# Asking for ScalarE's rounding of a weight unit four tiles later in a two-block transformer kernel

## The reference

```
mod = silu(c) @ w_ada + b_ada                      # scale, shift and gate vectors
h = rmsnorm(x)*(1+sc)+sh;  p = h @ w_in            # 2048 -> 9296 columns
y_a = latent attention(p) @ w_o_mla                # 8 heads, softmax
y_b = gated delta rule(conv4+silu(p)) @ w_o_gdn    # chunks of 64
x += gt * ((g_a*y_a + g_b*y_b) @ w_o)
x += gt * ((silu(h@w_gate) * (h@w_up)) @ w_down);  x = rmsnorm(x)
# second block
p = rmsnorm(x) @ w_in_2                            # a, gate, q, k, v
mix = concat(conv31+layernorm+silu(a*sigmoid(gate)), windowed attention(q,k,v)) @ w_out_2
x += rmsnorm(mix);  x += rmsnorm(relu(rmsnorm(x)@w_up_2)^2 @ w_down_2)
```

## Time and profile before

| | |
|---|---:|
| median of three runs | 2861.0 us |
| the runs | 2860.99, 2861.0, 2869.02 us |
| span of the profiled execution | 2856.0 us |
| what lies around the span, taken as median less span | 5.0 us |
| PE busy | 96% |
| DVE busy | 71% |
| ACT busy | 48% |
| DMA | 565.31 MB, mean 198 GB/s |
| instructions | 43985 |

### The profile page before, as it was taken

The page is one execution under the profiler, slowest core; times in us unless marked ns, Lnnn a source line. Parts: engine busy times, 40 slices in busy tenths (PEclk is TensorE's granted clock), DMA queues, the critical chain, the costliest instruction groups (busy, mean ns, idle before and its releaser), DMA issues.

```text
span 2856.0 us, 43985 instructions
## 1 busy us (share of the span) xinstructions
PE 2747.0 (96%) x17404; PEld 2439.8 (85%) x17404; DVE 2033.0 (71%) x2983; ACT 1360.4 (48%) x2169; POOL 208.1 (7%) x180
## 2 busy tenths in 40 slices
PE   6988999999999999999999999999999999999997
PEld 6888778888889888888888889998788888888886
DVE  7898786777797886555556688996567566575665
ACT  3445653343444544444444554465654444444454
POOL 0231000000002000000000080111110000000001
PEclk9999999999999999999999999999999999999999
DMA  9864255656787686555555555554445555555553
GB/s 392 314 228 134 95 172 186 198 192 206 236 304 268 217 305 226 191 188 188 191 185 192 187 169 169 177 165 139 153 130 182 190 187 191 187 190 189 188 190 127
DMA packets 158461, 565.31 MB, mean 198 GB/s; under 512 B 17584, under 2 KB 21936, under 8 KB 158256
## 3 DMA queue, kind: packets, MB, share of 16 engines
q1 hardware_dynamic: 158256, 562.50, 58.9%
HBM read 560.33 MB, written 2.10 MB: 197 GB/s over the span
## 4 chain that ended last, share of the span: by engine, by line
PE 85%; DVE 9%; ACT 3%; issue 2%; DMA 1%; SPq 0%; POOL 0%; DVEq 0%; ACTq 0%; POOLq 0%
PE BK L350 20%; PE BK L348 19%; PE BK L351 10%; PE BK L347 10%; PE BK L353 6%; PE BK L355 5%; PE BK L354 5%; DVE LO L657 2%; PE BK L435 2%; ACT HI L517 1%; DVE ADA L653 1%; DVE B L865 1%; DVE B L707 1%; PE BK L360 1%; PE BK L461 1%
## 5 line engine op out<-in xcount | busy, mean ns | idle before, releaser
L517 ACT ACTIVATE HI<-RAW 128x1024 fp32r<-128x1024 f32 x825 | 875.1, 1061 | 1253.7 <-PE BK L348 862.3
L657 DVE TENSOR_TENSOR LO<-RAW,HI 128x1024 fp32r<-128x1024 f32 x825 | 1017.9, 1234 | 376.2 <-ACT HI L517 373.0
L350 PE MATMUL BK<-H,HI 128*128 128x512 f32 x2528 | 1009.5, 401 | 9.0 <-DVE LO L657 8.5
L348 PE MATMUL BK<-H,HI 128*128 128x512 f32 x2496 | 985.3, 396 | 0.0
L351 PE MATMUL BK<-H,LO 128*128 128x256 f32 x2528 | 703.0, 278 | 0.0
L347 PE MATMUL BK<-H,LO 128*128 128x256 f32 x2496 | 698.2, 280 | 0.4 <-DVE H L703 0.2
L353 PE MATMUL BK<-H,HI 128*128 128x256 f32 x1840 | 545.6, 296 | 33.6 <-DVE B L707 15.7
L347 PEld LDWEIGHTS BK<-H,LO 128*128 128x128 f32 x2496 | 469.7, 188 | 111.8 <-DVE H L703 2.0
L351 PEld LDWEIGHTS BK<-H,LO 128*128 128x128 f32 x2528 | 477.0, 189 | 99.7 <-issue 1.0
L354 PE MATMUL BK<-H,HI 128*128 128x256 f32 x1840 | 523.8, 285 | 0.0
L355 PE MATMUL BK<-H,LO 128*128 128x256 f32 x1840 | 523.6, 285 | 0.0
(11 more groups left out here) (244 smaller groups left out, 1870.5 us busy)
## 6 DMA issues: line engine op xcount, KB each, us to landing
RAW<-wst_dram SPq DMA_DIRECT2D x825, 512.0 KB, 3.9
RAW<-wada_dram SPq DMA_DIRECT2D x155, 512.0 KB, 4.5
EARLY<-wada_dram SPq DMA_DIRECT2D x37, 512.0 KB, 7.8
EARLY<-wst_dram SPq DMA_DIRECT2D x33, 512.0 KB, 6.7
X<-xT_dram SPq DMA_DIRECT2D x8, 512.0 KB, 8.8
B<-bias_dram SPq DMA_DIRECT2D x32, 128.0 KB, 3.4
out_dram<-X SPq DMA_DIRECT2D x3, 512.0 KB, 2.7
CN<-consts_dram SPq DMA_DIRECT2D x1, 840.0 KB, 8.1
```

Source lines behind the costliest of these rows:

```text
L348: e.matmul(bk[:, :], hh, H[:, k, :], start=False, stop=last, skip_group_check=True).then_inc(S["tile"], 1)
L350: e.matmul(bk[:, :], hh, H[:, k, :], start=first, stop=False, skip_group_check=True)
L517: e.activation(HI[:, u % NHL, :], raw_at(slot), ACT.Copy).then_inc(S["hi"], 1)
L657: e.tensor_tensor(LO[:, u % NHL, :], raw_at(slot), HI[:, u % NHL, :].bitcast(f32), sub).then_inc(S["lo"], 1)
```

## The change

`feed` loses its last lines, which asked for HI of unit u+3 at u.7 (in its own counting `u` is already the unit two ahead). They become a function of their own, called behind the flush of tile 3. At (u+1).3 it asks for the same unit, u+3. The rounding, its operands, its waits and LO's place at (u+1).7 stay as they are. On ACT's queue HI(u+3) is now behind the steps flushed at u.7, behind what stands at u.7+, and behind the flushes (u+1).1 and (u+1).3.

```diff
@@ feed(u)
                 while st["proc"] <= lin_at[u]:
                     proc_next()
+
+            def hi_ahead(u):
                 v = len(hi_tok)
-                if v <= u + 1 and v < len(lin_at) and st["load"] > lin_at[v] and (v < NHL or v - NHL in unit_pe):
+                if v <= u + 2 and v < len(lin_at) and st["load"] > lin_at[v] and (v < NHL or v - NHL in unit_pe):
                     hi_part(v)
@@ blocks(...)
                         elif i % 2 == 1:
                             w.flush()
+                            if i == 3:
+                                hi_ahead(u)
```

## The result

The changed kernel takes **2875.5 us** (median of 6 runs, 2872.8 to 2878.2) against 2861.0 (6 runs, 2857.4 to 2869.0): a ratio of 1.0051 with a 95% interval of 1.0039 to 1.0062, so 14.5 us slower. Its profiled execution has a span of 2874.2 us, 18.2 more than before. That is more than 14.5 because the profiled execution of before was a quick one: around the span lie 1.8 us after the change (2876.0 less 2874.2) and 1.7 to 2.1 us in the other runs of before, not the 5.0 taken ahead of the prediction, so that execution took about 2858 us, 3 less than its median. The queues of PE and DVE hold the same instructions in the same order as before; only ACT's order differs.

What follows compares the result with a forecast made beforehand. TensorE was busiest at 96%, with DVE full in short convolution and softmax. Terms -4.6 - 2 + 8 + 24 + 2 + 0 = +27.4 us on 2856.0, plus 5.0 around it, gave 2888 us, range 2866 to 2903.

Steps and rivals of the forecast that it cites:

- the copy behind HI: First pass: PE waits for a copy queued behind HI on ACT; moving HI ends that wait, -4.6 us.
- the later LO on a full DVE: Short convolution and softmax: HI behind ACT's work delays LO on a full DVE, +8 and +24 us.
- First passes and other waits: First pass -4.6 us (bounds 0 to -5); PE's bank waits, splits and copies at stage ends -2 (0 to -6).
- Short convolution: Turn from 3.81 to about 4.74 us; 6.5 us up to 290 us, 1.5 later; +8, bounds +4 and +15.
- Softmax: Long convolution with softmax: DVE waits for exponential and HI in every such unit; +24 us, bounds +8 and +29.
- the 19 delays: Softmax stretch: LO delayed at each of 19 exponentials, mean 1.54 us, 29.3 us before deductions.
- The four delays: Softmax stretch: LO's delays worked out from records, +1.97, +2.14, +1.37 and +0.69 us.
- DVE's rest and a lead of 3: Softmax stretch: taken off 29.3 us, DVE's idle 2.2 us and LO's estimated lead over PE of 3.
- w_o_gdn: HI behind a split on ACT delays LO about 1 us in some four units, half counted; +2, bounds 0 and +4.
- Feed-forward: Feed-forward parts: later HI still ends ahead of LO, with a cover of 2.6 us; costed at nothing.
- Attention and delta rule: First block, 300 to 780 us: ACT's results earlier, DVE's later; taken as 0, bounds -5 and +8.
- the busiest-engine view: Whole kernel: a shift within ScalarE's queue changes nothing, 2861 us; same time as the no-change rival, chance 0.07.

Runs made afterwards that it cites:

- run 3: The changed kernel with the old place (u.7, ahead of the flush) for units 58 to 75, the short convolution; 2862.6 us, ratio 1.0009 to before.
- 4: The kernel before with the new place in units 0 to 53 alone, the first passes; 2852.5 us, ratio 0.9971 to before.
- run 5: The kernel before with the new place in units 76 to 177 alone, first block's attention and delta rule; 2847.7 us, ratio 0.9957 to before.
- run 6: The kernel before with one single HI, that of unit 107, at its new place; 2855.2 us, ratio 0.9986 to before.
- 7: Long-convolution taps 16 to 30 left out, two per unit instead of four: changed kernel 2849.9 us (0.9965), kernel before 2852.7 us (0.9975).
- 1: The changed kernel with HI(u+3) asked for right behind the flush at u.7 in every unit; 2844.1 us, ratio 0.9942 to before.

## Why the prediction came out as it did

The forecast was slower, 2888 us in a range of 2866 to 2903; it is 2875.5, and slower: 14.5 us where 27.4 were forecast. The two large mechanisms, the copy behind HI and the later LO on a full DVE, are as forecast. That the total lies inside the range, and by half a us in the band given to the forecast itself (2875 to 2900), is in part luck, since a gain of 13.3 us that was not foreseen met a price of the short convolution that was 5.1 us too small. The terms, one by one:

- *First passes and other waits, -4.6 and -2.* Measured -5.6, and -8.1 with this part alone. The mechanism is as forecast, and the wait for line 521 is gone. Of it -3.1 fell by LO 17, and the rest in the second and third pass, which the prediction had under "other waits". There is no sign that DMA took over: its share is 0.92 in a window with PE at 54.00 of 54.
- *Short convolution, +8.* The turn is 4.82 us as forecast (4.74). Up to 290 us (LO 70) the stage lost 6.3, as priced (6.5). The term was too small because the next six turns, up to LO 76, cost another 6.8 us, where all later turns were put at 1.5. In the turns behind those (LO 76 to 88) the loss doesn't grow further (-0.3 us), in run 3 as well (-0.3), where they alone have the new place. So turns that cost nothing are there, as the prediction said, but they begin six turns later; that PE's fp32 work is what covers them was not tested. The 13.1 us are inside the bounds of 4 and 15.
- *Softmax, +24.* Measured 23.4, and the run with the old place in this stretch alone gave 20 back. The mechanism and the 19 delays are as forecast, but the close agreement is luck. The four delays were put at 1.97, 2.14, 1.37 and 0.69 us and came to about 1.89, 1.9, 0.92 and 0.63; the 19 units grew by 25.3 us together, not by 29.3. And only 2.0 us came back in the other units, where 5.2 (DVE's rest and a lead of 3) were taken off: two errors that cancel. What the prediction did not say is that ACT and DVE form a loop, of which HI becomes a part.
- *w_o_gdn, +2.* Measured 4.5, but 1.5 to 2.5 show also in the runs that have the old place there (4, 5, 6 and 7). So 2 to 3, in the bounds.
- *Feed-forward, 0.* -1.2 and -1.3, within what executions differ by. LO's stops there rose by 177.1 us, both releasers taken together, and moved nothing, as said.
- *Attention and delta rule, 0 with bounds of -5 and +8.* **This is the step that failed**, "No row prices it; I bound it by -5 and +8 and take 0, as DVE is not full there". Measured -13.3, and with this part alone 13.3 us in the median (8.6 to 15.7). A row did price it: PE's waits for line 835, 7.4 us in 3 times. The longest of them, followed back, leads in three steps to an exponential behind a waiting HI. This is the mechanism that the prediction had found in the first pass, with a copy in the exponential's place. The two stalls of 3.10 and 3.04 us went to 1.0 or less and took their dips of the clock with them. The rest of the 13.3 wasn't taken apart: some 1.4 is a dip in the profile of before between 564 and 576 us (granted clock 0.86) that no stall precedes and that runs 1, 4, 6 and 7, with the old place there, also lack, and the other steps come with shorter waits.

Of the rivals, the busiest-engine view gave 2861, 14.5 us too low. Engine shares of the whole kernel (96, 71 and 48%) were the same before and after to one point, while stages moved by -13 to +23 us. The advice of the Trainium skill, "Perfetto Trace Analysis", section "Optimization Strategy", to take a regime by itself, find the gaps on its engine and ask which semaphore ends them, is the one that these runs bear out: followed for the 3.10 us gap at 487.63 us it leads to the HI of unit 107.

## What to carry to other kernels

In this kernel the best place for an instruction that must wait was behind work that is ready and ahead of work that waits for another engine, except in the delta rule, where still later was better. Where it is placed behind something that waits for its own consumer's queue, two engines close into a loop, and the cost is what that loop takes beyond the bound engine's time for a unit, once per turn. So look for the best place stage by stage: here one rule for the whole kernel cost 14.5 us, and two rules by stage won 25.5. And price every row of PE's waits, also the short ones: 7.4 us in 3 times pointed at a gain of 13.

## What the runs showed of the hardware

Three stalls of TensorE in the profile of before, of 3.10 us (from 487.63), 2.61 us (from 352.02) and 3.04 us (from 660.75), were each followed by a lower granted clock, that is, by a part of the time at 1.2 instead of 2.4 GHz. The windows of the last two:

```profile
352.00:360.00 8.00, 5.39 (x32) 5.13 (x32) 6.74 (x17) 5.36 (x13) 0.00 (x0) 0.79 0.19 69
```
```profile
656.00:676.00 20.00, 16.96 (x111) 15.44 (x110) 14.77 (x20) 6.04 (x10) 0.00 (x0) 0.91 0.52 166
```

Of 12, 8 and 20 us that leaves 1.7, 1.7 and 1.8 us of clock lost, the first window being the one shown with the run of one HI, so that a stall of about 3 us with its dip costs about half as much again as it shows. The two of 3.10 and 3.04 us were followed by a dip in every profile that has them (four and five of the twelve). The one of 2.61 us was not: in run 6 it is there again, 2.61 us from 351.35, and so is one of 2.50 us from 351.00 in run 5, and in both the granted clock is 1.00 (from 350 to 366 us in run 6, from 340 to 366 us in run 5). With the stall of 3.10 us cut to 0.56 us the dip was gone. The dip of before between 564 and 576 us, with PE busy all the time and no stall of over 0.9 us in the 70 us ahead of it, shows that a stall isn't the only thing that leads to one; what did there stays open.
